# The attention branch of a two-layer mixer: scores issued three ahead in four banks, keys of two heads in one product, queries of layer 1 for half of the tokens

## The reference, cut to what matters

```python
def mla_qkv(z, g_cq, w_uq, g_ckv, w_uk, w_uv, rope):
    c_q, c_kv, k_rope = jnp.split(z, (384, 640), axis=-1)
    q = (rmsnorm(c_q, g_cq) @ w_uq).reshape(B, T, 8, 64 + 32)
    c_kv = rmsnorm(c_kv, g_ckv)
    k_nope = (c_kv @ w_uk).reshape(B, T, 8, 64)
    v = (c_kv @ w_uv).reshape(B, T, 8, 64)
    ...
def attend(q, k, v):
    s = jnp.einsum('bqhd,bkhd->bhqk', q, k).astype(jnp.float32) * (64 + 32) ** -0.5
    p = jax.nn.softmax(s, axis=-1).astype(v.dtype)
    return jnp.einsum('bhqk,bkhd->bqhd', p, v)
```

## Time and profile before

| | |
|---|---|
| median of 3 runs | 3030.55 us (3027.95 to 3035.78) |
| the profiled execution | 3029.15 us, its span 3027.3 us |
| TensorE busy | 2633.2 us, 87% |
| VectorE, ScalarE, GpSimd busy | 28%, 20%, 6% |
| mean granted TensorE clock | 0.93 |
| HBM read | 604.87 MB, 216 GB/s over the span |

### The profile page before, as it was taken

One profiled execution on the slowest core, in us unless ns is written; L12 is line 12 of the kernel. 1 busy time (PEld: TensorE's weight loads), 2 busy tenths in 40 slices (PEclk: granted clock), 3 DMA queues, 4 the chain that ended last, 5 costly groups with the idle time before them and its releaser, 6 DMA issues.

```text
span 3027.3 us, 38844 instructions
## 1 busy us (share of the span) xinstructions
PE 2633.2 (87%) x15968; PEld 1426.5 (47%) x15968; DVE 852.4 (28%) x1977; ACT 604.5 (20%) x1176; POOL 170.7 (6%) x178
## 2 busy tenths in 40 slices
PE   6868989899998899899897587998899899878884
PEld 3335647654445444344343333637778743323233
DVE  1233444521114431111112422435531422111114
ACT  3232431220002011111110223422220211111110
POOL 0000000000000111111110000000000011111110
PEclk8999989999997899999999799999999889998997
DMA  6010013331202499999996501103223389999993
GB/s 280 21 56 7 29 56 142 137 116 59 80 0 94 172 361 423 394 415 402 379 398 256 221 21 56 35 28 113 94 104 139 127 334 390 424 419 416 415 399 144
DMA packets 74560, 617.39 MB, mean 204 GB/s; under 512 B 17678, under 2 KB 17678, under 8 KB 32016
## 3 DMA queue, kind: packets, MB, share of 16 engines
q1 hardware_dynamic: 50192, 564.52, 45.9%
q0 software_dynamic: 24192, 50.39, 4.4%
HBM read 604.87 MB, written 47.71 MB: 216 GB/s over the span
## 4 chain that ended last, share of the span: by engine, by line
PE 81%; DVE 7%; DMA 4%; issue 4%; ACT 3%; SPq 0%; POOLq 0%; DVEq 0%; ACTq 0%; POOL 0%
PE bank L1711 20%; PE bank L1726 9%; PE bank L1197 8%; PE bank L286 6%; PE bank L356 3%; PE bank L1212 3%; PE bank L1202 3%; PE bank L1701 3%; DMA arena<-expert_rows 2%; PE bank L377 2%; PE bank L397 1%; PE bank L915 1%; PE bank L415 1%; PE bank L930 1%; PE bank L258 1%
## 5 line engine op out<-in xcount | busy, mean ns | idle before, releaser
L1711 PE MATMUL bank<-ring,arena 128*64 128x512 f32 (+1 forms) x1648 | 589.2, 627 | 100.2 <-issue 94.4
L1711 PEld LDWEIGHTS bank<-ring,arena 128*64 128x64 f32 (+1 forms) x1648 | 204.3, 157 | 424.3 <-issue 423.2
L1711 PE MATMUL bank<-branches,arena 128*64 128x512 f32 (+1 forms) x528 | 259.8, 649 | 0.0
L1197 PE MATMUL bank<-normed,ring 128*128 128x512 f32 (+1 forms) x768 | 255.5, 486 | 0.0
L1889 DVE TENSOR_TENSOR arena<-bank,arena 128x256 f32<-128x256 f32 x83 | 35.3, 425 | 705.8 <-ACT arena L1813 705.8
L1635 POOL DMA_INDIRECT arena<-hidden_rows,block_slots x81 | 82.5, 1018 | 2411.4 <-DVE block_slots L1464 1803.6
L286 PE MATMUL bank<-normed,ring 128*128 128x512 f32 x448 | 194.4, 593 | 0.0
L1197 PEld LDWEIGHTS bank<-normed,ring 128*128 128x128 f32 x768 | 145.9, 190 | 102.2 <-issue 92.3
L1813 ACT ACTIVATE arena<-bank 128x256 f32<-128x256 f32 x83 | 31.9, 385 | 688.3 <-PE bank L1711 688.3
L1726 PE MATMUL bank<-ring,arena 128*64 128x512 f32 (+1 forms) x560 | 163.4, 597 | 1.3 <-DVE arena L1895 1.3
L1726 PE MATMUL bank<-arena 128*64 128x512 f32 (+1 forms) x528 | 138.3, 597 | 1.1 <-ACT arena L1816 1.1
(11 more groups left out here) (430 smaller groups left out, 3606.2 us busy)
## 6 DMA issues: line engine op xcount, KB each, us to landing
ring<-in_wexp SPq DMA_DIRECT2D x96, 2048.0 KB, 20.2
ring<-in_wst SPq DMA_DIRECT2D x54, 2048.0 KB, 8.4
branches<-in_wexp SPq DMA_DIRECT2D x34, 2048.0 KB, 11.4
ring<-in_wexp SPq DMA_DIRECT2D x66, 1024.0 KB, 22.7
arena<-in_wexp SPq DMA_DIRECT2D x64, 1024.0 KB, 21.7
arena<-expert_rows SPq DMA_DIRECT2D x12, 2048.0 KB, 7.3
ring<-in_wst SPq DMA_DIRECT2D x4, 1536.0 KB, 11.3
hidden_rows<-arena SPq DMA_DIRECT2D x6, 512.0 KB, 2.9
```

The lines of the kernel that those rows point to most:

```text
L1197: last = nc.tensor.matmul(ps[2 * (n % 4)][:, c0:], wg[:, k, i * P:(i + 1) * P], H[:, k, c0:], start=(k == 0), stop=(k == KD - 1))
L1711: last = nc.tensor.matmul(ps[2 + s][r0:r1, :], XT_[:, s, k * P + r0:k * P + r1], wt[:, k, :], start=(k == 0), stop=(k == KD - 1))
```

## The change

Four things change, all in the first branch.

1. Order of the projections: latents 0 to 3, first sum of squares, latents 4 and 5, second sum, then the queries, which wait for the first three scalings only; the copy of the rotary key stands behind the first query. ScalarE and VectorE follow that order.
2. Keys: four products of 128 columns of weights, two heads each, in place of eight of 64. ScalarE evicts each in two copies, and that of the odd head goes from partitions 64 to 127 to partitions 0 to 63.
3. Layer 1: latents 0 to 2, the first sum, its root, the scalings of the query latents, and the queries and their evictions take columns 256 to 511 only.
4. Loop: scores are issued three units ahead, into banks 6, 7, 2 and 5 in turn, with four buffers of probabilities `Pb`; the weighing is two units behind the flips, and `pair_out` stands one unit later.

The core of the diff:

```diff
-        Pb, PT = arena(0, 2, 512), arena(1024, 2, 512)
+        Pb, PT = arena(0, 4, 512), arena(2048, 2, 512)
+        SCORE_BANK, FLIP_BANK = (6, 7, 2, 5), (3, 4)
...
+        def queries_from(l):
+            return 0 if l == 0 else TC
...
-                    last = nc.tensor.matmul(ps[j][:, :], w[:, k, (j % 4) * P:(j % 4 + 1) * P], H[:, k, :], start=(k == 0), stop=(k == KD - 1))
+                    last = nc.tensor.matmul(ps[j][:, c0:], w[:, k, (j % 4) * P:(j % 4 + 1) * P], H[:, k, c0:], start=(k == 0), stop=(k == KD - 1))
...
+            for j in range(4):
+                latent(j)
+            mean_square(0, 0, 3)
+            latent(4)
+            latent(5)
+            mean_square(1, 3, 5)
...
-            pe.wait_ge(mla["zn"], l * MLA["zn"] + 5)
-            for j in range(20):
+            pe.wait_ge(mla["zn"], l * MLA["zn"] + 3)
+            for j in range(16):
                 if j >= 13:
-                    pe.wait_ge(mla["kve"], l * MLA["kve"] + j - 5 - 7)
+                    pe.wait_ge(mla["kve"], l * MLA["kve"] + j - 12)
                 elif j >= 5:
                     pe.wait_ge(mla["qe"], l * MLA["qe"] + j - 4)
+                if j == 8:
+                    pe.wait_ge(mla["zn"], l * MLA["zn"] + 5)
...
-                elif j < 16:
+                elif j < 12:
                     for k in range(2):
-                        last = nc.tensor.matmul(ps[j % 5][0:64, :], ukv[:, 0, k, (j - 8) * 64:(j - 7) * 64], Z[:, 3 + k, :],
-                                                start=(k == 0), stop=(k == 1))
+                        last = nc.tensor.matmul(ps[j % 5][:, :], ukv[:, 0, k, (j - 8) * P:(j - 7) * P], Z[:, 3 + k, :], start=(k == 0), stop=(k == 1))
...
+                if j == 0:
+                    pe.wait_ge(mla["kr"], l * MLA["kr"] + 1)
+                    nc.tensor.matmul(ps[5][64:128, :], cn("dup", 64)[0:64, :], KP[0:64, :], start=True, stop=True).then_inc(mla["kr"], 1)
...
             def score(u):
                 h, q, nk = units[u]
-                if u >= 2:
-                    pe.wait_ge(mla["ex"], l * MLA["ex"] + u - 1)
-                nc.tensor.matmul(ps[6 + u % 2][:, 0:nk * P], qT[:, h, q * P:(q + 1) * P], kT[:, h, 0:nk * P],
-                                              start=True, stop=True).then_inc(mla["s"], 1)
+                if u >= 4:
+                    pe.wait_ge(mla["ex"], l * MLA["ex"] + u - 3)
+                nc.tensor.matmul(ps[SCORE_BANK[u % 4]][:, 0:nk * P], qT[:, h, q * P:(q + 1) * P], kT[:, h, 0:nk * P],
+                                 start=True, stop=True).then_inc(mla["s"], 1)
...
-            score(0)
+            for u in range(3):
+                score(u)
             for u in range(U):
-                if u + 1 < U:
-                    score(u + 1)
+                if u + 3 < U:
+                    score(u + 3)
                 flip(u)
-                if u >= 1:
-                    weigh(u - 1)
+                if u >= 2:
+                    weigh(u - 2)
+            weigh(U - 2)
             weigh(U - 1)
...
+            for j in range(4):
+                square(j)
+            root(0, QL)
+            square(4)
+            root(1, KVL)
             act.wait_ge(mla["kr"], l * MLA["kr"] + 2)
             nc.scalar.activation(kT[64:128, :, :], bcast(ps[5][64:128, :], 1, HEADS), ACT.Copy).then_inc(mla["kr"], 1)
...
+                if j < 12:
+                    for odd in range(2):
+                        last = nc.scalar.activation(kT[0:64, 2 * (j - 8) + odd, :], ps[j % 5][64 * odd:64 * odd + 64, :], ACT.Copy)
...
+                if u >= 4:
+                    act.wait_ge(mla["t"], l * MLA["t"] + u - 3)
+                nc.scalar.activation(Pb[:, u % 4, 0:nk * P], ps[SCORE_BANK[u % 4]][:, 0:nk * P], ACT.Exp,
+                                     bias=st_nm[:, u:u + 1], accum_out=st_sum[:, u:u + 1]).then_inc(mla["ex"], 1)
                 if u >= 2:
-                    act.wait_ge(mla["t"], l * MLA["t"] + u - 1)
...
-                if u >= 1:
-                    copy_flipped(u - 1)
+                    copy_flipped(u - 2)
+            copy_flipped(U - 2)
             copy_flipped(U - 1)
...
-                if u >= per + 2 and (u - 2) % per == 0:
-                    pair_out((u - 2) // per - 1)
+                if u >= per + 3 and (u - 3) % per == 0:
+                    pair_out((u - 3) // per - 1)
```

More of the change, by code:

```diff
@@ L344, in units_mla, with latent @@
             return [(h, q, 2 if q < 2 else 4) for h in range(HEADS) for q in range(4) if l == 0 or q >= 2]
+        def queries_from(l):
+            return 0 if l == 0 else TC
         def mla_pe(pe, l):
-            for j in range(6):
+            q0 = queries_from(l)
+            def latent(j):
                 n = CH_MLA + j // 4
@@ L361, in mla_pe, with mean_square @@
-            for g, (j0, j1) in enumerate(((0, 3), (3, 5))):
+            def mean_square(g, j0, j1):
+                c0 = q0 if g == 0 else 0
                 pe.wait_ge(mla["zev"], l * MLA["zev"] + j1)
                 for j in range(j0, j1):
-                    last = nc.tensor.matmul(ps[6 + g][:, :], ones, ZSQ[:, j, :], start=(j == j0), stop=(j == j1 - 1))
+                    last = nc.tensor.matmul(ps[6 + g][:, c0:], ones, ZSQ[:, j, c0:], start=(j == j0), stop=(j == j1 - 1))
                 last.then_inc(mla["ss"], 1)
-            pe.wait_ge(mla["zn"], l * MLA["zn"] + 5)
@@ new lines, in root @@
+            def root(g, n):
+                c0 = q0 if g == 0 else 0
+                act.wait_ge(mla["ss"], l * MLA["ss"] + g + 1)
+                ch.link(nc.scalar.activation(RSL[:, g, c0:], ps[6 + g][:, c0:], ACT.Ln, scale=1.0 / n, bias=cn("eps", 1)))
+                nc.scalar.activation(RSL[:, g, c0:], RSL[:, g, c0:], ACT.Exp, scale=-0.5).then_inc(mla["rs"], 1)
+            for j in range(4):
[3 more added lines that the diff above has]
+            root(1, KVL)
@@ L434, in mla_act @@
             act.wait_ge(mla["kr"], l * MLA["kr"] + 2)
             nc.scalar.activation(kT[64:128, :, :], bcast(ps[5][64:128, :], 1, HEADS), ACT.Copy).then_inc(mla["kr"], 1)
-            for g, n in enumerate((QL, KVL)):
-                act.wait_ge(mla["ss"], l * MLA["ss"] + g + 1)
-                ch.link(nc.scalar.activation(RSL[:, g, :], ps[6 + g][:, :], ACT.Ln, scale=1.0 / n, bias=cn("eps", 1)))
-                nc.scalar.activation(RSL[:, g, :], RSL[:, g, :], ACT.Exp, scale=-0.5).then_inc(mla["rs"], 1)
@@ L440, in mla_act @@
-            for j in range(8, 20):
-                act.wait_ge(mla["p"], l * MLA["p"] + j + 1)
-                if j < 16:
-                    nc.scalar.activation(kT[0:64, j - 8, :], ps[j % 5][0:64, :], ACT.Copy).then_inc(mla["kve"], 1)
+            for j in range(8, 16):
+                act.wait_ge(mla["p"], l * MLA["p"] + j + 1)
+                if j < 12:
+                    for odd in range(2):
+                        last = nc.scalar.activation(kT[0:64, 2 * (j - 8) + odd, :], ps[j % 5][64 * odd:64 * odd + 64, :], ACT.Copy)
+                        if odd:
+                            last.then_inc(mla["kve"], 1)
+                        else:
+                            ch.add(last)
```

55 lines of the change are left out of this document (30 added, 25 removed).

## The result

The kernel after the change takes 2908.15 us (median of 4 runs, 2904.81 to 2912.04), against 3032.73 for the kernel before beside it (4 runs): a ratio of 0.9591, with a 95% interval of 0.9572 to 0.961 (the brackets behind the ratios below are such intervals too). Forecast were 2912 us, with a range of 2902 to 2932. The profiled execution took 2912.04, with a span of 2910.1.

A forecast was written before the change was run, and what follows sets the result against it. TensorE was taken as the bound (81% of the span). Projections 18.1 and 37.8 plus loops 40.1 and 22.1 sum to 118.1 us off the profiled 3029.15, giving 2911.1; the median was put at 2912, range 2902 to 2932.

The forecast's parts named there:

- the marks 1453.0 and 1142.5: Lengths in us of the stages behind the branch in layers 0 and 1; longer ones would mean time given back.
- Projections, layer 0: Layer 0 before the loop: fewer key instructions (6.9), closed holes and better clock save 18.1 us.
- 9.3 + 2.0 less small change: Layer 0 projections: 9.3 us of idle holes closed, 2.0 us of lower clock behind them removed, less shape-change costs.
- Projections, layer 1: Layer 1 before the loop: layer 0's 18.1 plus halved query-side columns, less 0.5 for clock, saves 37.8 us.
- The second root: Layer 1 projections: risk that it delays TensorE; claimed covered, first query out 1.1 us before it is wanted.
- The loop: Attention loops: scores three ahead remove waits, TensorE sets the pace; gains of 40.1 us in layer 0, 22.1 in layer 1.
- the gap of 0.45 us a unit: Attention loops: TensorE time lost between score, flip and weighing groups, 14.4 us for layer 0's 32 units.
- the lower bound of 0.37: Attention loops: smallest gap in us a unit allowed for, taking 4 us off the forecast time.
- (a): Attention loop keeps a wait of 0.5 us in each of 48 units, giving 24 back: 2936 us; chance 13%.
- (b): Stages behind the branch: two late weight chunks give back 17 us: 2929 us; chance 4%.
- (d): Attention loop unchanged, for instance because early scores wait for the Exp that frees their bank: 2974 us; chance 1%.
- (c): New branch: TensorE's 223 us of work runs at the 1.2 GHz clock and takes twice that: 3135 us; chance 2%.

The follow-up runs named there:

- e4: Kernel after with keys of one head a product (eight products of 64 columns, one eviction each): median 2921.91 us, ratio 0.9644.
- e3: Kernel after with the old order of the projections (six latents, key copy, both sums, all scalings, then queries): median 2931.18 us, ratio 0.9681.
- e2: Kernel after with layer 1's query side over all 512 columns again: median 2928.04 us, ratio 0.9666.
- group 6: Kernel after with loop units taken in pairs (two scores, two flips, two weighings; four buffers of flipped probabilities): medians 2892.51 and 2898.48 us.
- e6: Kernel after with one added ScalarE copy of the score tile a unit, ahead of its Exp: median 2905.08 us, ratio 0.959.
- e7: Kernel after with three added ScalarE copies of the score tile a unit, ahead of its Exp: median 2914.99 us, ratio 0.9622.
- e9: Kernel after, unchanged, once more: median 2901.72 us, ratio 0.9584.
- e1: Kernel after with the old attention loop (scores one unit ahead in two banks, weighing one behind): median 2978.55 us, ratio 0.9822.
- e10: The kernel after with the old attention loop, unchanged, once more: 2982.34 us, one run.

## Why the prediction was right, by its steps

**Bounds.** That TensorE sets the pace and that what the branch gives up moves all that follows held: the middle and end stages kept their length within their own spread. They were not below the marks 1453.0 and 1142.5 in the first profile (1457.8 and 1143.9), which by the prediction's own sign would be time given back; the second, with 1454.7 and 1135.9, is 4.9 below the marks in sum. The sign was too sharp for stages whose sum spreads by 15 us.

**Projections, layer 0** (18.1; measured 18.7). Keys 6.9: e4 has 7.2. The order with its holes and its clock, 9.3 + 2.0 less small change: e3 has 10.9. The first score came 84.4 us after the first latent, forecast 84.9.

**Projections, layer 1** (37.8; measured 38.9). The columns are right to 0.1 in each term (e2). Latent 0 is paced as forecast: ScalarE begins its copy of it 7.5 us after the first product, and the forecast had it end after 7.3. The order is worth 13.5 here and not 11.3, since more of the stretch at the lower clock lies behind the hole in layer 1 (e3); undone one at a time the three edits sum to 40.4, 1.5 more than together. The second root was never near its limit. ScalarE, kernel after, layer 0:

```profile
98.18 1.28 ACT L462 ACT_TABLE_LOAD   x1
105.67 0.69 ACT L462 ACTIVATE arena<-bank,consts 128x512 f32<-128x512 f32 x1 [6.20 <-PE bank L371]
106.37 1.28 ACT L463 ACT_TABLE_LOAD   x1
107.66 0.63 ACT L463 ACTIVATE arena<-arena 128x512 f32<-128x512 f32 x1
```

The first load stands ahead of the wait for the sum and starts 7.5 us before that wait ends, so a root takes 108.3 - 105.7 = 2.6 us after its sum, not 3.9. By the prediction's steps that makes its slack of 1.1 us one of 2.4. In ScalarE: Activation LUTs, What ACT_TABLE_LOAD costs, the Trainium skill gives a switch 2.66 us with its drain; from the end of Ln at 106.36 to the start of Exp at 107.66 it is 1.30, and the measurement decides.

**The loop** (40.1 + 22.1; measured 43.3 + 24.4). The mechanism was right: the flips' idle time fell from 36.9 us in the loop of layer 0 to 0.3, and TensorE's own pace is the length. That TensorE alone sets the pace leaves one term to size, and it was sized too large: the gap of 0.45 us a unit. It measured (62.97 - 51.8) / 32 = 0.35 and (39.40 - 34.5) / 16 = 0.31. Score to flip is 148.69 - 147.73 - 0.86 = 0.10 (taken: 0.14), weighing to score 0.15 (taken: 0.15), and flip to weighing 149.22 - 148.69 - 0.43 = 0.10 (taken: 0.16, from groups whose flips had just waited). The 0.10 between score and flip is no trait of these two: it is gone where no weighing stands before the score (group 6). The difference, 0.10 x 32 + 0.14 x 16 = 5.4 us, is all by which the loops did better; the lower bound of 0.37 was not low enough. The profiled time hides it, as the untouched stages were 8.0 longer in that execution; the medians side by side differ by 124.6 us, 6.5 more than the 118.1 forecast.

**Rivals.** (a), a wait kept: no, one of 0.32 us in layer 0 and one of 0.25 at the end of layer 1; e6 shows one ScalarE operation a unit to spare and e7 where it would have come true. (b), given back by a transfer: no (e9); a chunk lands in 7.7 us. (d), scores that wait for their bank: no, and e1 gives its price, some 2980 and not 2974. (c), the clock: not in this kernel, though e7 lost some 2 us to it. But the reason given against it, that the old loop was granted 1.00 throughout, does not carry over to other projections: e1 and e10 have the same loop of layer 0 at 0.50 for 16 us. The forecast was right to give (c) little, with a reason weaker than it looked.

## What to carry to other kernels

Where one engine is the bound and waits once per unit on a chain through two others, run two units ahead; a third buys little (here 2.3 us), and after that the changes of tile width are what is left, which pairing halves. A hole can cost more than its length, since the clock may be down behind it: 9.3 and 10.2 us of idle time (both waits together) cost 10.9 and 13.5. Judge a small loss in untouched stages only by a second profile of the same kernel; what makes those stages of one kernel differ by up to 12.7 us here (2659.2 and 2646.5) was not found.

## What the runs showed of the hardware that was not expected

- The same loop, with TensorE busy 1.2 of the first 2.5 us, was granted 1.00 in one kernel and fell to 0.50 for some 16 us in another, in both of its profiled executions (5.9 us).
- The clock fell inside a hole of 8.51 us and inside one of 9.37, and was down for some 10 us both times; 4.5 and 6.2 us of that came behind the hole.
- It also fell in a loop over four banks whose idle stretches were at most 1.44 us (e7), and in none over four banks with hardly any idle time.
- A change between products of 128*128 and 128*64 tiles takes 0.10 to 0.16 us on TensorE, and the first 128*128 score behind a weighing costs 0.10 more; groups of one tile width follow each other with 0.01 us or less between them.
- ScalarE's table load runs ahead of the wait of the activation that it belongs to, so that of two loads a root one is free.
